# Time mixing's group norm: values centred per head where PE turns them to tokens, gate and weights applied ahead of the root, operand split by quarters

## The reference

```python
def rwkv7_time_mix(h, ..., ln_w, ln_b, w_o):          # H = 16 heads of N = 64
    ...
    def step(state, inp):                             # over the 256 tokens
        sa = jnp.einsum('bhij,bhj->bhi', state, -kk_t)
        state = (state * w_t[:, :, None, :] + sa[..., None] * b_t[:, :, None, :]
                 + v_t[..., :, None] * k_t[:, :, None, :])
        y = jnp.einsum('bhij,bhj->bhi', state, r_t)
        return state, y
    ...
    mean = jnp.mean(y, axis=-1, keepdims=True)
    var = jnp.mean(jnp.square(y - mean), axis=-1, keepdims=True)
    y = ((y - mean) * lax.rsqrt(var + GN_EPS)).reshape(B, S, C)
    y = y * ln_w + ln_b
    bonus = jnp.sum(r_h * k_h * r_k, axis=-1, keepdims=True) * v_h
    y = (y + bonus.reshape(B, S, C)).astype(h.dtype)
    return (y * g) @ w_o
```

## Time and profile before

| | |
|---|---|
| Time, three executions | 2098.1, 2097.89, 2097.32 us; median 2097.89 us |
| The profiled execution's own time | 2099.99 us |
| Its span, first to last instruction | 2098.0 us |
| Mean granted TensorE clock | 0.972 |
| Busy | PE 1948.2 us (93%), DVE 1333.0 (64%), ACT 1057.5 (50%), POOL 55.4 (3%) |

### The profile page before, as it was taken

The page is one execution under the profiler, slowest core; times in us unless marked ns, Lnnn a source line. Parts: engine busy times, 40 slices in busy tenths (PEclk is TensorE's granted clock), DMA queues, the critical chain, the costliest instruction groups (busy, mean ns, idle before and its releaser), DMA issues.

```text
span 2098.0 us, 43614 instructions
## 1 busy us (share of the span) xinstructions
PE 1948.2 (93%) x18356; PEld 1899.4 (91%) x18356; DVE 1333.0 (64%) x1651; ACT 1057.5 (50%) x1376; POOL 55.4 (3%) x44
## 2 busy tenths in 40 slices
PE   6999997899998999998999699999999798999998
PEld 5998997799998999997887699999999797999998
DVE  6586579577777755798443656556555646556555
ACT  5555565655556444576422545445444455445443
POOL 0020000000000000000160000000000000000000
PEclk9999998899999999999999899999999899999999
DMA  5743332154553455443301234554455353334553
GB/s 203 219 165 139 121 122 101 66 196 162 190 188 141 162 184 184 152 161 126 137 4 43 83 121 179 180 180 175 171 186 185 125 181 121 143 133 166 182 184 115
DMA packets 51880, 313.35 MB, mean 149 GB/s; under 512 B 13488, under 2 KB 13616, under 8 KB 14256
## 3 DMA queue, kind: packets, MB, share of 16 engines
q1 hardware_dynamic: 51328, 308.42, 41.2%
q10 hardware_dynamic: 432, 3.15, 0.4%
HBM read 310.50 MB, written 1.05 MB: 148 GB/s over the span
## 4 chain that ended last, share of the span: by engine, by line
PE 69%; DVE 18%; ACT 6%; issue 4%; DMA 1%; DVEq 0%; ACTq 0%; SPq 0%
PE ps L281 61%; DVE wl L1892 5%; ACT wh L1265 2%; PE ps L760 2%; DVE pages L2329 1%; DVE work L1921 1%; DMA raw<-in_stream 1%; DVE pages L2149 1%; DVE pages L2391 1%; DVE pages L2151 1%; DVE pages L1965 1%; DVE pages_r L1909 1%; PE ps L939 1%; PE ps L746 1%; DVE pages L2185 1%
## 5 line engine op out<-in xcount | busy, mean ns | idle before, releaser
L1892 DVE TENSOR_TENSOR wl<-raw,wh 128x1024 fp32r<-128x1024 f32 x576 | 700.9, 1231 | 541.0 <-ACT wh L1265 539.1
L1265 ACT ACTIVATE wh<-raw 128x1024 fp32r<-128x1024 f32 x576 | 598.3, 1052 | 466.6 <-PE ps L281 426.8
L281 PE MATMUL ps<-sq_r,wh 128*128 128x256 f32 x2592 | 743.7, 287 | 15.3 <-DVE h_r L1909 8.3
L281 PE MATMUL ps<-sq_r,wl 128*128 128x256 f32 x2592 | 736.8, 284 | 0.0
L281 PE MATMUL ps<-h_r,wh 128*128 128x256 f32 x2560 | 727.9, 284 | 0.0
L281 PE MATMUL ps<-pages_r,wh 128*128 128x256 f32 x2480 | 548.9, 287 | 48.9 <-DVE pages_r L1909 34.6
L281 PEld LDWEIGHTS ps<-sq_r,wh 128*128 128x128 f32 x2592 | 501.2, 193 | 20.1 <-issue 16.1
L281 PEld LDWEIGHTS ps<-sq_r,wl 128*128 128x128 f32 x2592 | 501.0, 193 | 0.0
L281 PEld LDWEIGHTS ps<-h_r,wh 128*128 128x128 f32 x2560 | 495.2, 193 | 0.5
L281 PE MATMUL ps<-pages_r,wl 128*128 128x256 f32 x1680 | 479.7, 286 | 0.0
L281 PEld LDWEIGHTS ps<-pages_r,wh 128*128 128x128 f32 x2480 | 426.4, 196 | 53.1 <-issue 42.0
(11 more groups left out here) (308 smaller groups left out, 1826.2 us busy)
## 6 DMA issues: line engine op xcount, KB each, us to landing
raw<-in_stream SPq DMA_DIRECT2D x288, 1024.0 KB, 4.8
pages<-in_rpb SPq DMA_DIRECT2D x32, 64.0 KB, 5.9
pages<-in_mem SPq DMA_DIRECT2D x1, 1024.0 KB, 4.9
x<-in_x SPq DMA_DIRECT2D x1, 1024.0 KB, 12.7
pages<-in_mem ACTq DMA_DIRECT2D x1, 1024.0 KB, 5.0
pages<-in_gmlp_b ACTq DMA_DIRECT2D x1, 1024.0 KB, 4.7
pages<-in_gmlp_w ACTq DMA_DIRECT2D x1, 1024.0 KB, 6.8
out<-h SPq DMA_DIRECT2D x4, 256.0 KB, 2.5
```

The source lines that it names most:

```text
L281: mm = pe.matmul(out, left, right, start=start and q == 0, stop=stop and q == 2, skip_group_check=True)
L1265: f(t.wh[(2 * b0 + hf) % PIECE_SLOTS][:], t.raw[b0 % 2][:, hf * 1024:(hf + 1) * 1024], ACT.Copy).then_inc(s["high_done"], 1)
L1892: tt(t.wl[i][:], t.raw[b0 % 2][:, hf * 1024:(hf + 1) * 1024], t.wh[i][:].bitcast(F32), ALU.subtract).then_inc(s["low_done"], 1)
```

## The change

The mean is no longer computed from `y`. A new 128x128 matrix `t.centre`, the identity minus 1/64 of `head_ones`, is made on DVE by one instruction, early in time mixing. `turn_tokens(8..11)` multiplies the tiles of values by it, in 16 plain f32 matmuls, where 16 transposes by the identity stood. Since `y` is linear in the values, it arrives centred in PSUM. The bonus still uses the values as they were.

The copy of `y` (L1779), the head sums (L900) and the subtraction (L2532) are gone; ACT squares straight from PSUM. A one-column Ln of a constant stands ahead of ACT's wait for `rw_yt`. The two 1 MB DMAs move behind the four Exp. DVE forms `(bonus + ln_b) * gate` before `y` is there and `y * ln_w * gate` while the squares are summed; after the root only a product and a sum per quarter are left. `operand_low` is split into quarters that stand between the quarters of the norm.

```diff
@@ -184,6 +184,7 @@
         t.stat = sb("stat", [P, 48])
         t.lb = sb("lb", [P, 48])
         t.pc = sb("pc", [P, KT * NCH])
+        t.centre = sb("centre", [P, P])
         t.zrow = ctx.enter_context(nc.sbuf_tensor("zrow", [P, P], mybir.dt.bfloat16))
         t.ps = ctx.enter_context(nc.psum_tensor("ps", [P, 8, 512], F32))
         s = {n: ctx.enter_context(nc.semaphore(n)) for n in SEM_NAMES}
@@ -676,13 +677,18 @@
             pe.wait_ge(s["rw_dec"], 1)
         if q == 8:
             pe.wait_ge(s["u_evac"], SEG["rw_v"] + 4)
+            pe.wait_ge(s["rw_centre"], 1)
         if q < 4:
             pe.wait_ge(s["rw_bonus_sb"], q + 1)
         else:
             pe.wait_ge(s["rw_t_sb"], q - 3)
         for c in range(4):
-            mm = pe.transpose(ps[:, 4 + q % 4, c * P:(c + 1) * P],
-                              src[:, (c0 + c) * T + b * P:(c0 + c) * T + (b + 1) * P], cst(t, "ident"))
+            made = ps[:, 4 + q % 4, c * P:(c + 1) * P]
+            tokens = src[:, (c0 + c) * T + b * P:(c0 + c) * T + (b + 1) * P]
+            if q >= 8:
+                mm = pe.matmul(made, tokens, t.centre[:], start=True, stop=True)
+            else:
+                mm = pe.transpose(made, tokens, cst(t, "ident"))
         mm.then_inc(s["rw_t"], 1)
 
     project("rw_v", mix_parts(t, "rw_v"), n=2, name="rw_v")
@@ -895,10 +901,6 @@
     for turn in range(2):
         pe.wait_ge(s["rw_turn"], turn + 1)
         read_tokens(turn).then_inc(s["rw_yt" if turn else "rw_turn"], 1)
-    for q in range(4):
-        pe.wait_ge(s["rw_yt_sb"], q + 1)
-        pe.matmul(ps[:, 4 + q, :], cst(t, "head_ones"), t.page[8][:, q * 512:(q + 1) * 512],
-                  start=True, stop=True).then_inc(s["rw_mean"], 1)
     for q in range(4):
         pe.wait_ge(s["rw_sq"], q + 1)
         pe.matmul(ps[:, 4 + q, :], cst(t, "head_ones"), t.sq[:, q * 512:(q + 1) * 512],
@@ -1771,16 +1773,10 @@
           ACT.Copy, scale=-1.0).then_inc(s["rw_rhs_sb1"], 1)
         act.wait_ge(s["rw_u1"], n_ + 1)
         f(t.page[4][po, b * D + 512:(b + 1) * D], ps[po, 5, :], ACT.Copy).then_inc(s["rw_u_sb1"], 1)
+    f(t.stat[:, 42:43], t.stat[:, COL_EPS:COL_EPS + 1], ACT.Ln)
     act.wait_ge(s["rw_yt"], 1)
-
-    act.dma_start(t.page[5], a.bias_rows).then_inc(s["rows_in"], 16)
-    act.dma_start(t.page[9], a.mix_weights).then_inc(s["rows_in"], 16)
     for q in range(4):
-        f(t.page[8][:, q * 512:(q + 1) * 512], ps[:, q, :], ACT.Copy).then_inc(s["rw_yt_sb"], 1)
-    for q in range(4):
-        c = slice(q * 512, (q + 1) * 512)
-        act.wait_ge(s["rw_cent"], q + 1)
-        f(t.sq[:, c], t.page[8][:, c], ACT.Square).then_inc(s["rw_sq"], 1)
+        f(t.sq[:, q * 512:(q + 1) * 512], ps[:, q, :], ACT.Square).then_inc(s["rw_sq"], 1)
     for q in range(4):
         c = slice(q * 512, (q + 1) * 512)
         act.wait_ge(s["rw_var"], q + 1)
@@ -1790,6 +1786,8 @@
         act.wait_ge(s["rw_varsb"], q + 1)
         f(t.page[2][:, c], t.page[2][:, c], ACT.Exp, scale=-0.5).then_inc(s["rw_std"], 1)
 
+    act.dma_start(t.page[5], a.bias_rows).then_inc(s["rows_in"], 16)
+    act.dma_start(t.page[9], a.mix_weights).then_inc(s["rows_in"], 16)
     operand_high("rw_o", t.page[7], t.page_r[10], lambda q: act.wait_ge(s["rw_out"], q + 1))
     highs("rw_o", n=3)
 
@@ -2395,6 +2393,7 @@
         operand_low(name, plain, high_, low_)
 
     mixed("rw_k")
+    stt(t.centre[:], cst(t, "head_ones"), -1.0 / RW_D, cst(t, "ident"), ALU.mult, ALU.add).then_inc(s["rw_centre"], 1)
     lows("mem2_k", 2, 2)
     link(dve.memset(t.work[64:P, 0:T], 0.0))
     dve.memset(t.work[0:64, T:2 * T], 0.0).then_inc(s["inner_zero"], 1)
@@ -2526,22 +2525,30 @@
         if n_ < NCH - 1:
             new_state(n_, 0)
             new_state(n_, 1)
-    for q in range(4):
-        c = slice(q * 512, (q + 1) * 512)
-        dve.wait_ge(s["rw_mean"], q + 1)
-        stt(t.page[8][:, c], ps[:, 4 + q, :], -1.0 / RW_D, t.page[8][:, c], ALU.mult, ALU.add).then_inc(s["rw_cent"], 1)
-    for q in range(4):
+    for k in range(KT):
+        c = slice(k * T, (k + 1) * T)
+        ins = stt(t.page[0][:, c], t.page[0][:, c], par(t, "rwkv_ln_b_2", k), t.page[13][:, c], ALU.add, ALU.mult)
+    link(ins)
+    for k in range(KT):
+        c = slice(k * T, (k + 1) * T)
+        if k % 2 == 0:
+            dve.wait_ge(s["rw_sq"], k // 2 + 1)
+        ins = stt(t.page[8][:, c], ps[:, k // 2, k % 2 * T:(k % 2 + 1) * T], par(t, "rwkv_ln_w_2", k), t.page[13][:, c],
+                  ALU.mult, ALU.mult)
+    link(ins)
+
+    def normed(q):
+
         c = slice(q * 512, (q + 1) * 512)
         dve.wait_ge(s["rw_std"], q + 1)
         link(tt(t.page[8][:, c], t.page[8][:, c], t.page[2][:, c], ALU.mult))
-        for k in (2 * q, 2 * q + 1):
-            ck = slice(k * T, (k + 1) * T)
-            ins = ts(t.page[8][:, ck], t.page[8][:, ck], par(t, "rwkv_ln_w_2", k), par(t, "rwkv_ln_b_2", k),
-                     ALU.mult, ALU.add)
-        link(ins)
-        link(tt(t.page[8][:, c], t.page[8][:, c], t.page[0][:, c], ALU.add))
-        tt(t.page[7][:, c], t.page[8][:, c], t.page[13][:, c], ALU.mult).then_inc(s["rw_out"], 1)
-    operand_low("rw_o", t.page[7], t.page_r[10], t.page_r[7])
+        tt(t.page[7][:, c], t.page[8][:, c], t.page[0][:, c], ALU.add).then_inc(s["rw_out"], 1)
+
+    for q in range(4):
+        normed(q)
+        if q:
+            operand_quarter("rw_o", t.page[7], t.page_r[10], t.page_r[7], q - 1)
+    operand_quarter("rw_o", t.page[7], t.page_r[10], t.page_r[7], 3)
     residual("rw_o", then="x0")
 
     def memory_heads(i, query):
```

More of the change, by code:

```diff
@@ L124 @@
 rw_kkln rw_kkvar rw_kkn rw_bonus_in rw_bonus_sum rw_bonus_sb rw_cum rw_exp rw_dec rw_t rw_t_sb rw_lx rw_mb rw_rk rw_lt rw_lx_read rw_xx
-rw_plain rw_masked rw_lm rw_y rw_y_sb rw_z rw_z_sb rw_rhs0 rw_rhs1 rw_rhs_sb0 rw_rhs_sb1 rw_u0 rw_u1 rw_u_sb0 rw_u_sb1
-rw_ds0 rw_ds1 rw_s0 rw_s1 rw_turn rw_yt rw_yt_sb rw_mean rw_cent rw_sq rw_var rw_varsb
+rw_plain rw_masked rw_lm rw_y rw_y_sb rw_z rw_z_sb rw_rhs0 rw_rhs1 rw_rhs_sb0 rw_rhs_sb1 rw_u0 rw_u1 rw_u_sb0 rw_u_sb1 rw_centre
+rw_ds0 rw_ds1 rw_s0 rw_s1 rw_turn rw_yt rw_sq rw_var rw_varsb
 rw_std rw_out fin_gain fin_log fin_inv fin_log2 fin_logs fin_std gm_vnorm gm_vstd gm_vout0 gm_vout1 gm_mask gm_mix gm_mixed
```

## The result

| | before | changed |
|---|---|---|
| Median | 2097.61 us (4 executions, 2096.8 to 2098.1) | 2082.99 us (4 executions, 2081.37 to 2084.6) |
| The profiled execution's own time, its span | 2099.99 us, 2098.0 | 2084.6 us, 2082.5 |
| Mean granted TensorE clock | 0.972 | 0.978 |

The ratio is 0.9931, 95% interval 0.9918 to 0.9944: 14.6 us faster, and the forecast was 13.9. The changed kernel run again gave 2084.58 us (6 executions, 2081.8 to 2086.5) against 2096.4 for the kernel before beside it, 11.8 us faster, ratio 0.9942, 0.9925 to 0.9959. One execution of the kernel before there, at 4799.8 us, is left out as far outside.

The account below looks back on a forecast made before the run. Bound by one chain that PE, ACT and DVE hand each other through the group norm, 26.6 us. 7.4 + 8.65 - 1.85 - 0.25 = 13.95 us off the 2097.89 median gives 2084.0 us, range 2081.3 to 2088.0.

Parts of the forecast that it names:

- The head of the norm: From the reads of y to DVE's first product: it starts at 1150.5 in place of 1157.88, 7.4 us gained.
- The tail: From DVE's first product to PE's projection: 3.5 us in place of 12.15, 8.65 us gained.
- The DMA issues did lie under Exp: ACT's DMA issues before the first rounding: taken to cost 0 under table load and Exp, 0.7 us as other end.
- The matrix: Making t.centre by one DVE instruction in a run wholly on the chain: 0.25 us paid, between 0.17 and 0.4.
- The turning: Turning the values by plain products, 3.55 us, in place of transposes, 1.70: 1.85 us paid, counted whole.
- the turning is free: Rival: PE's unnamed 2.92 us pause behind the chunk matrices takes up the extra matmuls; 2082.1 us, chance 0.10.
- the signs of being wrong: Clock falls at sums, DMA issues delay first rounding, a low part waits for ACT, or pause behind chunk matrices changes length.
- The sum: Whole kernel: 7.4 + 8.65 - 1.85 - 0.25 = 13.95, about 13.9 us gained, 2084.0 us.
- The rival of the clock in the sums: PE's clock halves in the sums of squares, 1.8 us less gained; with DMA issues 2085.8 to 2086.5; chance 0.25.
- The projection's stream was not broken: Projection behind the norm: low parts by quarters arrive in time, every 1.95 us, so PE's stream is not broken.
- the slower case: Rival: quarters break PE's stream, the projections stay at half clock; 25.3 us lost, 11.4 net, 2109.3 us, chance 0.02.

Follow-up runs that it names:

- Experiment 3: The kernel before with only ACT's part: Ln's table loaded during ACT's wait for y, the two DMAs behind the four Exp; 2093.34 us, ratio 0.9982.
- experiment 6: The changed kernel without the one-column Ln, so Ln's table loads between the squares and the first Ln; 2083.55 us, ratio 0.9933.
- Experiment 2: The kernel before with only DVE's part: products formed early, two instructions a quarter behind the root, low part by quarters; 2087.27 us, ratio 0.9946.
- experiment 7: The changed kernel with the four low parts behind all four quarters, as before the change; 2086.3 us, ratio 0.9949.
- experiment 4: The changed kernel with the values turned by transposes, so the mean is not removed from y; 2082.39 us, ratio 0.9925.
- experiment 10: The changed kernel with each of the 16 products that turn the values issued twice; 2087.66 us, ratio 0.9962.
- Experiment 5: The changed kernel with the two DMA issues back ahead of ACT's squares; 2086.0 us, ratio 0.9948.
- experiment 11: The changed kernel with DMA issues ahead of the squares and two filling products on PE between reads and sums; 2082.37 us, ratio 0.9934.
- experiment 1: The kernel before with only the centring folded into the turning of the values, head sums and subtraction gone; 2095.21 us, ratio 0.9991.

## Why the prediction was right, step by step

**The head of the norm, 7.4 us: right as the chain of the new kernel, too high by 1.7 where the clock does not fall.** From the first square to DVE's first product were 1151.43 - 1144.31 = 7.1 us (7.0 forecast), and that product stands 7.3 us nearer to the last read than in the trace of before. But 1.7 of these are the clock fall in that trace's head sums; against an execution without it the head is worth 5.7. Experiment 3 shows the issues and the table load, experiment 6 the load alone at 0.73 of its 1.28 us, since PE's sums are what Ln waits for.

**The tail, 8.65 us: right.** PE follows DVE's first product by 3.50 us (3.5 forecast). Experiment 2 has the same 3.49 with everything else as before, and experiment 7 shows that the split by quarters is 2.7 of it. The DMA issues did lie under Exp, as taken.

**The matrix, 0.25 us: right in size.** In the chain of the changed kernel:

```profile
888.06 2.41 DVE pages_r L1907 x4
890.47 0.20 DVE centre L2396
890.67 4.54 DVE wl L1890 x4
```

**The turning, 1.85 us "counted whole": the size is right, its place on the path is not.** PE took 3.84 us in place of 1.97, 1.87 more, 32 instructions 0.12 us apart. The Trainium skill, "TensorE: Matmul & The Clock Gate", section "Terms", has a factor of four for the transpose mode in FP32. The traces have 1.9 for these tiles, and the measurement decides. DVE's wait for the first inverse grew by the whole 1.87 (4.28 in place of 2.41), but most of it did not carry through to the inversion. With transposes PE came to a stop of 2.3 to 3.0 us that ended 7.1 to 7.8 us after the turning began; with 16 plain products a stop of 0.9 to 1.3 us ended 7.3 to 7.8 us after it. About 0.5 to 0.7 us of the 1.87 show by the means of 4 and 9 traces (experiment 4), and the next 3.6 nearly whole (experiment 10). This lies between the forecast and the rival "the turning is free", nearer to the rival. It is one of the signs of being wrong that the prediction named: the pause behind the chunk matrices changed its length. What ends the stop is open. No record names a releaser, and that it is the arrival of instructions was not tried.

**The sum: close in part by luck.** G went from 26.79 to 10.85, 15.9 us; forecast were 16.05 for head and tail. Without the clock fall in the head sums it would be 25.1 - 10.85 = 14.2. With 0.2 for the matrix and 0.7 for the turning the chain gives 13.3 us without the fall and 15.0 with it. The profiled executions, that of before with the fall, differ by 15.4. The medians differ by 14.6 in the first set and by 11.8 in the second. So two errors stood against each other: the head was worked out from one execution with a clock fall in it, up to 1.7 us too much, and the turning was priced about 1.2 too high. How many executions of the kernel before have the fall is not known, since there is one trace of it. The medians do not tell 13.9 from the rival's 15.8.

**The rival of the clock in the sums** did not come in the changed kernel: the gap after the reads is 0.7 us, and PEclk was 1.00. Experiment 5 shows that it is real with the longer gap of 1.9 us, 1.7 us in size, though not in every execution (experiment 2); that filling the gap removes it rests on the one trace of experiment 11. The projection's stream was not broken, and no execution came near the slower case.

## What to carry to other kernels

- Where engines hand one chain to each other with nothing beside it, add up the chain's own steps. Head and tail, worked out from spacings of the rows, came out within 0.2 us each in the trace.
- A wait of the next engine shows that it is late, not that the path is. Ask what stops the third engine, and for how long, before an added microsecond is counted whole; here a stop of 3 us behind it took up about 1.2 of 1.9.
- One pair of traces can agree by chance. Two traces gave 15.81 and 15.83 us for plain products and transposes; thirteen showed a difference of 0.7, and a DVE instruction that had hidden it.
- A total over one execution holds clock stretches that the next one lacks. Compare a local measure from a fixed event to a fixed event, and read PEclk for it before a difference is put down to the edit.

## What the runs showed of the hardware

- PE's granted clock fell to its lower level (0.50, 1.2 GHz) in sums that followed a gap of 1.9 us in two traces (before, experiment 5), and not in a third with the same gap (experiment 2) nor in one with a gap of 3.8 us (experiment 1). With the gap filled by two products the sums took 3.60 us (experiment 11), and with a gap of 0.7 us they were at full clock in every trace. Eight f32 instructions of 512 columns took 3.60 to 3.71 us at full clock and 5.41 with the fall.
- Behind a stop of PE of 2.3 to 3.0 us the granted clock fell in three traces of four; behind one of 0.9 to 1.3 us at the same place in none of nine.
- A product of 128x128 by 128x128 in f32 took two instructions 0.12 us apart, 0.24 us in all; a transpose of the same tile one of 0.12.
- A DVE product of 128x2048 took 2.28 to 2.29 us in eleven traces. In the three where a POOL product (L2699 in the changed kernel) had begun 0.1 to 0.2 us before it, it took 3.35 to 3.36. That the two engines hold each other up is read from this overlap; no run was made for it.
- ACT's queue issued two 1 MB DMAs in 0.35 and 0.45 us under running Exp; in front, with nothing queued on ACT, they took 0.35 and 0.45 to 0.83, and ACT stood still for them.
- Executions of one program differed by up to 10.6 us in 2097 with no edit at all (2092.7 to 2103.3), while G repeated to 0.01 us in six traces.
